# Token rows of the expert mixtures fetched as four sub-rows and turned by DVE's 32x32 squares

## The reference

```python
def expert_block(args):          # mixture 1, k = 2, 32 experts
    xb, e = args
    hb = jax.nn.silu(xb @ w_gate[e]) * (xb @ w_up[e])
    return hb @ w_down[e]
...
wts = wts / wts.sum(-1, keepdims=True) * ROUTED_SCALE      # mixture 2, k = 8, 64 experts
...
def block_ffn(args):
    xb, e = args
    return (jax.nn.silu(xb @ w_gate[e]) * (xb @ w_up[e])) @ w_down[e]
yb = lax.map(block_ffn, (xin, blk_e)).reshape(NB * MOE_BLOCK, D)
y_assign = yb[dest] * sw[:, None].astype(yb.dtype)
routed = jax.ops.segment_sum(y_assign, stok, num_segments=T)
shared = (jax.nn.silu(xt @ ws_gate) * (xt @ ws_up)) @ ws_down
return (routed + shared).reshape(B, S, D)
```

## Time and profile before

| | us |
|---|---|
| median of 3 runs | 3336.09 |
| the runs | 3334.97, 3336.09, 3340.61 |
| span of the profiled execution | 3331.2 |
| what lies around the span | about 4.9 |
| PE busy | 3055.5 (92%) |
| DVE busy | 1832.3 (55%) |
| ACT busy | 1125.1 (34%) |
| POOL busy | 550.3 (17%) |

### The profile page before, as it was taken

How to read it: one execution, slowest core, us unless ns; L and a number is a source line. 1 busy time by engine, 2 the same in 40 slices (tenths; PEclk the granted TensorE clock), 3 DMA queues, 4 the chain that set the end, 5 groups by cost and what they waited for, 6 DMA issues and landing times. The chain is left out here.

```text
span 3331.2 us, 54837 instructions
## 1 busy us (share of the span) xinstructions
PE 3055.5 (92%) x17983; PEld 1496.7 (45%) x17984; DVE 1832.3 (55%) x3122; ACT 1125.1 (34%) x1385; POOL 550.3 (17%) x908
## 2 busy tenths in 40 slices
PE   8999989996999999499979998898899999999992
PEld 4444445553666444333337776344333333333330
DVE  3322244444777212444456775335388888788886
ACT  2222133333555100111113341121155555555554
POOL 1100000000000000011130000000155555455552
PEclk9999999997999999699979999998899999999996
DMA  6221021114231210699950011102397999899985
GB/s 238 93 97 44 0 89 51 51 51 98 52 77 52 76 71 32 246 387 421 421 191 26 25 38 66 67 32 86 155 333 241 353 378 371 269 333 321 316 261 183
DMA packets 177423, 557.32 MB, mean 167 GB/s; under 512 B 17436, under 2 KB 91776, under 8 KB 140160
## 3 DMA queue, kind: packets, MB, share of 16 engines
q1 hardware_dynamic: 140384, 424.31, 33.4%
q0 software_dynamic: 31968, 118.90, 13.1%
q10 hardware_dynamic: 4968, 12.74, 1.0%
HBM read 455.93 MB, written 99.98 MB: 167 GB/s over the span
## 5 line engine op out<-in xcount | busy, mean ns | idle before, releaser
L1977 PE MATMUL gu_ps<-w_gu,more 128*32 x1152 | 512.2, 598 | 17.2 <-DVE more L2129 7.7
L1982 PE MATMUL gu_ps<-h,more 128*32 128x512 f32 x1152 | 512.5, 598 | 0.0
L1982 PE MATMUL gu_ps<-second,more 128*32 128x512 f32 x1152 | 512.5, 598 | 0.0
L1982 PE MATMUL gu_ps<-more 128*32 128x512 f32 x1152 | 512.5, 598 | 0.0
L2010 PE MATMUL y_ps<-w_dn,hid_t 128*32 (+1 forms) x768 | 351.0, 600 | 4.4 <-DVE more L2117 2.4
L2015 PE MATMUL y_ps<-h,hid_t 128*32 128x512 f32 (+1 forms) x768 | 351.5, 601 | 0.0
L357 PE MATMUL front<-second,wcol 128*128 128x512 f32 x768 | 330.4, 592 | 4.8 <-ACTq L65 2.4
L2046 ACT ACTIVATE second<-w_gu 128x2048 f32 x148 | 275.0, 1905 | 120.8 <-issue 85.9
L2099 DVE COPY h<-w_gu 128x1024 f32 (+1 forms) x348 | 265.8, 770 | 77.9 <-issue 46.9
L1540 POOL COPY moe_idx<-moe_slot_tok 128x1 int32<-128x1 int32 x4 | 0.6, 189 | 1809.2 <-DVE moe_slot_tok L1708 1809.2
L1977 PEld LDWEIGHTS gu_ps<-w_gu,more 128*32 128x32 f32 x1152 | 121.7, 110 | 374.2 <-issue 374.1
(11 more groups left out here) (483 smaller groups left out, 5942.2 us busy)
## 6 DMA issues: line engine op xcount, KB each, us to landing
w_gu<-in_w_gate_dram SPq DMA_DIRECT2D x96, 1024.0 KB, 11.8
w_gu<-in_w_up_dram SPq DMA_DIRECT2D x96, 1024.0 KB, 15.4
w_dn<-in_w_down_dram SPq DMA_DIRECT2D x96, 1024.0 KB, 15.0
wcol<-in_w_in_dram SPq DMA_DIRECT2D x12, 1024.0 KB, 5.3
qk_by_head<-stage SPq DMA_DIRECT2D x32, 384.0 KB
qk<-qk_by_head SPq DMA_DIRECT2D x16, 768.0 KB
expert_rows<-h ACTq DMA_DIRECT2D x24, 512.0 KB
w_gu<-in_w_in_dram SPq DMA_DIRECT2D x20, 512.0 KB, 4.5
```

The lines of the kernel that those rows point to most:

```text
L1977: nc.tensor.matmul(gu_ps[0:SIZE, slot], x_t[:, c, 0:SIZE], w_gu[:, bass.ds(ws, 1), :, c, :].rearrange("p o g n -> p (o g) n"), start=c == ...
L1982: last = nc.tensor.matmul(gu_ps[at, slot], x_t[:, c, at], st_gu[a][:, :, c, :], start=c == 0, stop=c == C - 1)
```

## The change

Each token row now lies in `token_rows` as four sub-rows of 256 columns (in mixture 2 with the 64 shares behind each of them: 320 columns). A block's gather is four indirect DMAs instead of one (`gather_quads`). DMA number a fetches, for the 32 rows of partitions 32a to 32a+31, all four sub-rows: sub-row r goes to the 32 partitions of quadrant r. One DVE instruction then turns 32x32 squares and writes `x_t` directly, so PE's eight transposes, `x_ps` and the copy out of it go. The four lists of indices come in `dispatch` from four more small matmuls (`spread_ps`) and two DVE operations. ACT takes the shares; the last block has its own end in place of the dummy step; the hidden transposes move behind the down matmuls; the multiply on DVE comes after the first staging piece. The diff, cut:

```diff
+def gather_quads(g, G, rows_d, slot):
+    pieces = rows_d.rearrange("s (r n) -> (s r) n", r=QUADS)
+    for a in range(QUADS):
+        g.indirect_dma_start(G.xb[:, slot, a, :], None, pieces, bass.IndirectOffsetOnAxis(
+            ap=G.idx[:, slot, a:a + 1], axis=0)).then_inc(G.xb_in[slot], 16)
...
@@ dispatch
-                    sp.dma_start(rows_d[0:S, D:D + E].rearrange("(t p) e -> p t e", p=P), dense[:]).then_inc(dense_out, 16)
+                    for r in range(QUADS):
+                        sp.dma_start(quads[r][:, :, SUB:SUB + E], dense[:]).then_inc(dense_out, 16)
...
             for b in range(2):
-                g.indirect_dma_start(G.xb[:, b, :], None, rows_d, bass.IndirectOffsetOnAxis(
-                    ap=G.idx[:, b:b + 1], axis=0)).then_inc(G.xb_in[b], 16)
+                gather_quads(g, G, rows_d, b)
...
+            pe.wait_ge(spread_ready, 1)
+            pe.wait_ge(empty_ready, 1)
+            for a in range(QUADS):
+                last = nc.tensor.matmul(spread_ps[:, a, :], spread[:, a].rearrange("p r n -> p (r n)"), empty[:],
+                                        start=True, stop=True)
+            last.then_inc(spread_out, 1)
...
+            st(d.tensor_scalar(idx_f[:], spread_ps, float(QUADS), quad[:], ALU.mult, ALU.add))
+            st.join()
+            d.tensor_copy(G.slot_idx[:, 0:NB, :].rearrange("p b a -> p a b"), idx_f[:]).then_inc(slots_ready, 1)
@@ experts
             with eng.Fori(0, GROUPS) as j, ExitStack() as within:
                 for u in range(4):
                     i = j * 4 + (3 + u)
-                    within.enter_context(eng.If(i < n) if own_last else eng.If(i <= n))
-                    step(i, (3 + u) % 2, j * 32 + (16 + u // 2 * 16))
+                    within.enter_context(eng.If(i < n))
+                    step(i, (3 + u) % 4, j * 32 + (16 + u // 2 * 16))
...
             def gather(b, slot):
+                pool.wait_ge(x_ready, b - 1)
+                if not by_slot:
+                    pool.wait_ge(share_ready, b - 1)
...
-                g.indirect_dma_start(xb[:, slot, :], None, rows_d, bass.IndirectOffsetOnAxis(
-                    ap=idx[:, slot:slot + 1], axis=0)).then_inc(x_in[slot], 16)
-
-            def keep_share(b, slot, landed):
...
+                gather_quads(g, G, rows_d, slot)
...
@@ PE
-                if not first:
-                    turn_hidden(i)
-                turn_rows(i + 1, 1 - slot, 16 if first else rounds + 32)
-                if not first:
+                if not (isinstance(i, int) and i == 0):
                     finish(i)
+                turn_hidden(i + 1)
@@ ACT
+            def take_share(b, turn, landed):
+                a.wait_ge(x_in[turn % 2], landed)
+                for k in range(L):
+                    at = slice(k * SIZE, (k + 1) * SIZE)
+                    e = a.value_load(G.blk_e[0:1, k, bass.ds(b, 1)], min_val=0, max_val=E - 1)
+                    last = s.activation(share[at, turn:turn + 1], xb[at, turn % 2, k, bass.ds(e + SUB, 1)], ACT.Copy)
+                last.then_inc(share_ready, 1)
@@ DVE
+            def turn_x(slot):
+                d.transpose(x_t.rearrange("p c (a j) -> p a c j", j=QUARTER),
+                            xb[:, slot, :, 0:SUB].rearrange("p a (i c) -> p a c i", c=C)).then_inc(x_ready, 1)
...
-            def step(i, slot, rounds):
-                if not (isinstance(i, int) and i == 0):
-                    v.wait_ge(h_turned, i)
-                    d.tensor_copy(hid_t[:], h_ps).then_inc(h_ready, 1)
+            def step(i, turn, rounds):
+                slot = turn % 2
+                v.wait_ge(gu_ready, i + 1)
+                v.wait_ge(x_in[1 - slot], (i + 1) // 2 * 64 + 64 if isinstance(i, int) else rounds * 4 + 128)
+                turn_x(1 - slot)
+                stage_gate_up(i + 1, (0,))
                 v.wait_ge(silu_done, i + 1)
                 d.tensor_tensor(hid[:], act_g[:], gu_ps[:, slot, 1, :], ALU.mult).then_inc(hid_ready, 1)
-                v.wait_ge(x_turned, i + 2)
-                d.tensor_copy(x_t, x_ps[:]).then_inc(x_ready, 1)
-                stage_gate_up(i + 1)
...
+                stage_gate_up(i + 1, range(1, PIECES))
+                v.wait_ge(h_turned, i + 1)
+                d.tensor_copy(hid_t[:], h_ps).then_inc(h_ready, 1)
                 stage_down(i)
```

More of the change, by code:

```diff
@@ L48 @@
 LEAST = 3
+QUADS = 4
+SUB = D // QUADS
+WIDE2 = SUB + 64
 NB2 = (S * K2 // QUARTER + E2 * LEAST) // 4
@@ L340, in _ @@
             pool.wait_ge(cleared, 1)
-            for rows in spare:
-                pool.dma_start(rows[S:S + P, :], zero[:, 0:rows.shape[1]]).then_inc(zero_out, 16)
+            for rows, width in spare:
+                for c0 in range(0, width, D):
+                    w = min(D, width - c0)
+                    pool.dma_start(rows[S:S + P, c0:c0 + w], zero[:, 0:w]).then_inc(zero_out, 16)
             zero_rows(pool, sum_d, S + P, T + 1, zero[:, 0:D], zero_out)
@@ L345, in _ @@
             zero_rows(pool, y_d, S * K1, NB1 + 2 - S * K1 // P, zero[:, 0:D], zero_out)
-            pool.wait_ge(zero_out, 16 * (len(spare) + T + 1 + NB1 + 2 - S * K1 // P))
+            pool.wait_ge(zero_out, 16 * (sum(-(-width // D) for _, width in spare) + T + 1 + NB1 + 2 - S * K1 // P))
         @block.tensor
@@ L1777, in experts @@
         SIZE = P // L
-        share = ph.sb("share", [P, L, 2])
+        share = None if by_slot else ph.sb("share", [P, 4])
         xb, idx, mark = G.xb, G.idx, G.mark
@@ L1931, in later @@
-            def later(i, slot, rounds):
-                pool.wait_ge(x_turned, i)
-                if not by_slot:
-                    pool.wait_ge(share_in, i)
-                gather(i + 1, 1 - slot)
-                if not by_slot:
-                    scatter(i - 2, slot, rounds + 16, rounds + (16 + 16 * slot))
-                    keep_share(i, slot, rounds + 48)
+                if not by_slot and i >= 2:
+                    scatter(i - 2, i % 2, None, 16 if i == 3 else None)
             with pool.Fori(0, GROUPS) as j, ExitStack() as within:
@@ L1959, in _ @@
         def _(pe):
-            def turn_rows(b, slot, landed):
-                pe.wait_ge(x_in[slot], landed)
-                for c in range(C):
-                    last = nc.tensor.transpose(x_ps[:, c, :], xb[:, slot, c:D:C], G.ident[:])
-                last.then_inc(x_turned, 1)
-            def step(i, slot, rounds):
-                first = isinstance(i, int) and i == 0
+            def step(i, turn, rounds):
+                slot = turn % 2
                 e = pe.value_load(G.blk_e[0:1, 0, bass.ds(i, 1)], min_val=0, max_val=E - 1)
@@ L2056, in stage_down, with take_y, step @@
                              ACT.Copy).then_inc(act_d_staged, 1)
-            def step(i, slot, rounds):
+            def take_share(b, turn, landed):
[5 more added lines that the diff above has]
+                last.then_inc(share_ready, 1)
+            def take_y(b, to, turn):
+                a.wait_ge(y_ready, b + 2)
+                if by_slot:
+                    s.activation(to, y_ps[:], ACT.Copy).then_inc(y_taken, 1)
+                    return
+                a.wait_ge(share_ready, b + 1)
+                s.activation(to, y_ps[:], ACT.Copy, scale=share[:, turn]).then_inc(y_taken, 1)
+            def step(i, turn, rounds):
+                slot = turn % 2
+                first = isinstance(i, int) and i == 0
                 a.wait_ge(gu_ready, i + 1)
-                if not (isinstance(i, int) and i == 0):
+                if not first:
                     a.wait_ge(hid_ready, i)
@@ L2064, in step @@
                     stage_gate_up(i + 1)
-                if not (isinstance(i, int) and i == 0):
-                    a.wait_ge(y_ready, 1 + i)
+                if not by_slot:
+                    take_share(i + 1, (turn + 1) % 4,
+                               (i + 1) // 2 * 64 + 64 if isinstance(i, int) else rounds * 4 + 128)
+                if not first:
                     if not (isinstance(i, int) and i <= 2):
                         a.wait_ge(y_out[1 - slot], rounds)
+                    before = (turn + 3) % 4
+                    take_y(i - 1, y[:, 1 - slot, :], slice(before, before + 1))
                     if by_slot:
-                        s.activation(y[:, 1 - slot, :], y_ps[:], ACT.Copy).then_inc(y_taken, 1)
                         a.wait_ge(y_taken, 1 + i)
@@ L2073, in step @@
                         a.dma_start(to, y[:, 1 - slot, :]).then_inc(y_out[1 - slot], 16)
-                    else:
-                        a.wait_ge(share_ready, i)
-                        s.activation(y[:, 1 - slot, :], y_ps[:], ACT.Copy,
-                                     scale=share[:, 0, 1 - slot:2 - slot]).then_inc(y_taken, 1)
                 if ON_ACT:
@@ L2083, in _ @@
                 stage_gate_up(0)
-            steps(a, step)
+            if not by_slot:
+                take_share(0, 0, 64)
+            n = steps(a, step)
```

(6 more changed lines are left out.)

160 lines of the change are left out of this document (80 added, 80 removed).

## The result

The changed kernel takes 3458.78 us (median, 3456.23 to 3464.9), the kernel before 3336.74 us beside it: 1.0364 times as long, 95% interval 1.0351 to 1.0378. The forecast was 3355 with a range up to 3394; the change costs 122 us, not 19.

A forecast was written before the change was run, and what follows sets the result against it. PE and DMA both nearly full: weights set mixture 1, the gather's landing would hold mixture 2's steps near 11.9. Terms 8 + 5.5 + 2 + 6 - 8 + 8 - 2.4 = +19 on 3336.1 gave 3355 us, range 3314 to 3394.

The forecast's parts named there:

- Start of mixture 1: Before mixture 1: six more gather issues +8, small added operations +1.6, shorter tail -1.6; sum +8 us, bounds +5 and +9.6.
- Mixture 1: Mixture 1's loop, set by weight loads: gather packets +8, last two steps -1.8, dummy step -0.7; sum +5.5 us.
- the +8 for small packets: Mixture 1: 32 packets of 1 KB per engine instead of 8 of 4 KB, 24 x 0.34 = +8 us of DMA time.
- Start of mixture 2: Between the mixtures: additions mostly hidden by the shared unit's matmuls; PE's wait for slot numbers and spread matmuls cost +2 us.
- Mixture 2, DVE: Mixture 2's step: the turn takes 1.22 us, DVE about 10.4 with hand-overs, inside PE's 10.95.
- third rival: Mixture 2: the turn costs double, 2.45 us, DVE's step 11.6, total 3390 us; chance 0.08; its sign a turn over 2 us.
- Mixture 2, POOL: Mixture 2's step: four gather issues 5.4 us, the scatter and index copies make 9 to 10, under PE's 10.95.
- second rival: Mixture 2: POOL's gather issues stretch beside DVE's copies, steps of 12.5 to 12.7 us, total 3400 us; chance 0.13.
- the rival's price: Mixture 2, POOL: each gather issue beside DVE's copies at 1.82 us with gaps of 0.3, four making 8.5.
- Mixture 2, DMA: Mixture 2: the gather lands behind an expert's weights, closing steps at 11.8 to 11.95 us; load steps +6 us in all.
- the 32 packets of 1,280 bytes per engine: Mixture 2's gather: 32 small packets replace 8 of 4,352 B, +0.58 us a step, and alternate with all 24 weight packets.
- the sentence on the order of instructions: Mixture 2's step: the down matmuls' 3.5 us cover DVE's multiply; without that cover PE would stand the turn's 1.2 each step.

The follow-up runs named there:

- the repaired kernels: Changed kernel with DVE's multiply ahead of the turn and DVE's and PE's register reads ahead of their waits: 3382.0 us, ratio 1.0128; further variants build on it.
- one gather: Changed kernel with one indirect DMA of whole rows per block instead of four, three quarters of the sub-rows misplaced: 3463.2 us; on the split turn: 3339.4 us.
- the control with gathers earlier: Changed kernel with only POOL's gathers issued one step earlier, block i+2 ahead of the scatter of block i-2: 3420.1 us, ratio 1.0259.
- the split turn: The three-repairs kernel with DVE's turn in two halves and staging copies between them: 3341.3 us, ratio 1.0022; with gathers issued one step earlier 3298.6 us.
- multiply first: Changed kernel with DVE's multiply of the hidden layer ahead of the turn, and two staging calls made one: 3362.5 us, ratio 1.0090.
- PE's registers: Changed kernel with PE reading the next block's registers before it waits for the hidden rows, matmul order unchanged: 3381.8 us, ratio 1.0132.
- DVE's registers: Changed kernel with DVE reading the next block's expert numbers once, before its wait for gate/up, instead of twice behind it: 3414.2 us, ratio 1.0241.

## Why the prediction was wrong

- **Start of mixture 1**: +8 forecast, +9.0 measured; the row is the one at 1406.29 below, to hold against the earlier trace rows. Eight gathers are issued from 1387.74 to 1397.57, so that the six more are +7.5, as forecast. The rest fits by luck: the first issue comes 4.2 later (forecast: 1.6), the tail until the stage begins is 3.6 shorter (forecast: 1.6), and what follows until gate/up is 0.8 longer.

```profile
1387.74 1.06 POOL L1467 DMA_INDIRECT moe_xb<-token_rows,moe_idx  x1 [0.17 <-issue]
...
1396.62 0.95 POOL L1467 DMA_INDIRECT moe_xb<-token_rows,moe_idx  x1 [0.30 <-issue]
...
1406.29 1.11 PE L1998 MATMUL gu_ps<-w_gu,work 128*64 x1 [20.07 <-DVE work L2122]
```

- **Mixture 1**: +5.5 forecast, +5.2 in its loop. In the repaired kernels its median step falls to 10.9, while the loop stays at 292 to 294: that the loads set it holds. The number is right and its term wrong: the +8 for small packets is not there, since the rows come in packets of 4,096 bytes before and after, and queue 0 takes 10.8% in both the earlier trace rows. With one gather the loop was 298.8 in the changed kernel and 288.7 in the repaired one, so what makes the 5 us is open. Its end was missed: +7 from POOL's end of stage.
- **Start of mixture 2**: +2 forecast; of the 11.2 between the two loops about 8 had gathered when mixture 1 was left, and the rest is 3. About right.
- **Mixture 2, DVE**: the turn was taken at 1.22, within 0.69 to 2.45; it is 2.07. Nearer the upper bound, and over 2 us, the forecast's own sign for its third rival. Alone it explains little: replacing it by 0.69 gave nothing until the registers were out of the way.
- **Mixture 2, POOL**: 9 to 10 us a step forecast, and it had time left. The second rival falls: an issue in mixture 2 took 1.02 on average (1.10 over the whole kernel), and of 288 two took over 1.6. The Trainium skill's rule in "SBUF — State Buffer", section "Who interferes with whom", agrees in the control with gathers earlier: 143 issues lay beside a DVE copy and took 1.76 on average, 71 of them over 1.6, and the rest took 0.95. In the changed kernel only 71 of 285 lay beside a copy (1.18), the rest beside the turn or nothing (0.96 to 0.99), so that the rival's price was not paid. In the kernel before 70 of 72 lay beside a copy and took 1.02: which copies block an issue is not read from these runs.
- **Mixture 2, DMA**: the landing was forecast to close the step at 11.85 to 11.95. In the changed kernel it closed none (DVE waited 2.9 us for it, once). This step fails twice: something else closed the loop, and the 32 packets of 1,280 bytes per engine on which it rests were 8 of 5,120. Whether packets would take turns as the forecast has it is therefore not tested. Where the landing did show (the split turn), an earlier issue took most of the wait away.
- **The step that failed** is the sentence on the order of instructions: "DVE's multiply has the 3.5 us of the down matmuls as cover". The cover was compared with nothing. What has to fit under it is the turn with two register reads beside it and two copies: 3.4 to 4.5 us to the multiply's start, and then 1.46 of PE's queue, which has no matmul left to hide behind. The forecast gave the register reads of DVE and PE no price at all, though the edit put the one ahead of the multiply and uncovered the other; with the half clock in 27 steps this is the whole +99 (60 between the gate/ups, 40 in them). The runs price it: multiply first -88 of mixture 2, PE's registers -67, DVE's registers -50, each alone, and they overlap. The turn's own size, 2.07 for 1.22, has a part in it: by the forecast's numbers 1.22 and two copies fit under 3.5, and with the registers out of the way the longer turn costs 1.08 a step.
- **Rival 3** (DVE behind time, 3390) was nearest in kind, with the wrong reason: DVE's engine was not full, its queue was in the chain.
- **Slips in the sums**: rival 2 adds up to 3405, not 3400, and the chances to 0.57 slower and 0.14 the same. Neither changes the verdict.

## What to carry to other kernels

When an instruction is moved in front of a wait of another engine, add up all that stands between the releasing event and the wait, the queue's own work too: register reads, branches and waits are not in the busy times, but they lie in the chain as soon as no long work is queued behind them. Read registers before the wait, put the one instruction that another engine waits for first, and leave the bulk work behind it. And when a chain is shortened, look at once for what closed just behind it: here the gather, whose issue stood behind a scatter. Before a sum is built on the size of packets, look at what the trace records for them: four DMAs in place of one need not mean smaller packets.

## What the runs showed of the hardware

- A 32x32 turn of 1,024 float32 columns on 128 partitions took 2.07 us on DVE, of 512 columns 1.11; a plain copy of the same operand took 0.69.
- A register read from SBUF took 0.31 us on DVE's queue, and up to 1.65 in the 2 us after the end of a scatter's issue (108 of the 150 reads there took over 0.6, none of the 964 others).
- The rows of a block, fetched by four indirect DMAs of 32 rows x 4 sub-rows of 1,280 bytes each, were recorded in mixture 2 as 128 packets of 5,120 bytes, as they were with one DMA.
- In the control with gathers earlier a gather's issue on POOL took 0.95 us beside DVE's turn or beside nothing, and 1.76 on average beside DVE's copies (143 issues); in the kernel before it took 1.02 beside copies.
- POOL's end of stage after mixture 1 came 13.2 to 13.6 us after the last store's issue with four gathers to a block, and 6.4 to 7.0 with one.
- After idle times of 1.49 and 0.90 us on PE the granted clock was 0.50 for 3.4 us; after 0.70 and 0.96, in the step at 2815.80, and after 1.47 and 0.95, in the step at 2688.31, it stayed at 1.00. In the changed kernel 27 of 72 gate/up parts had such a stretch at half clock, in the kernel before 3.
